# The second attention by pairs of heads, features on partitions, and a row norm that is applied to the output product

## The reference

```python
proj = einsum('bsd,de->bse', x, w_in)
q, k, v, z_att, z_ssm, xbc, dt_raw = split(proj)          # 16 heads of 64
# three dilated windows (1, 4, 16) of causal attention with a bias by distance, merged by their lse
y_att = wts[0] * o1 + wts[1] * o2 + wts[2] * o3
y_att = rms_norm_2(y_att * silu(z_att), att_norm_g)       # over the 1024 features of a token
y_ssm = rms_norm_2(y * silu(z_ssm), ssm_norm_g)           # the state part, in the same way
mix = concatenate([y_att, y_ssm], axis=-1)                # 2048 features
out = einsum('bse,ed->bsd', mix, w_out)
x = layer_norm(alpha * x + out, ln_g, ln_b)
```

## Time and profile before

| | us |
|---|---|
| median of 3 runs (lowest, highest) | 2261.53 (2259.41, 2262.16) |
| the profiled execution, its own time | 2260.03 |
| its span, first to last instruction | 2258.2 |
| TensorE busy | 2044.2 (91%) |
| VectorE, ScalarE, GpSimd busy | 1319.2, 765.9, 613.6 |
| second attention, first scores to the last product | 1464 to 2038 |
| norm and turns behind it | 2038 to 2065 |
| output product | 2065 to 2230 |
| rest of layer norm, last store | 2230 to 2258 |

### The profile page before, as it was taken

One profiled execution on the slowest core, in us unless ns is written; L12 is line 12 of the kernel. 1 busy time (PEld: TensorE's weight loads), 2 busy tenths in 40 slices (PEclk: granted clock), 3 DMA queues, 4 the chain that ended last, 5 costly groups with the idle time before them and its releaser, 6 DMA issues.

```text
span 2258.2 us, 30694 instructions
## 1 busy us (share of the span) xinstructions
PE 2044.2 (91%) x12412; PEld 1246.1 (55%) x12412; DVE 1319.2 (58%) x2349; ACT 765.9 (34%) x1446; POOL 613.6 (27%) x623
## 2 busy tenths in 40 slices
PE   2999889988999988696998999899999999998994
PEld 2433345444444555244444665566776677677884
DVE  6328999999973464315455888455455545564005
ACT  3313434443216664113212443333333333333003
POOL 0031425541842023755322225012201220120110
PEclk8999989998999999897999999999999999999997
DMA  7110111221311212214111002001100110012101
GB/s 317 38 47 24 43 38 61 71 70 61 150 38 61 89 38 94 112 38 166 40 38 38 1 1 75 24 16 38 38 35 4 38 38 18 21 38 94 47 30 75
DMA packets 18542, 129.95 MB, mean 58 GB/s; under 512 B 1760, under 2 KB 1760, under 8 KB 13024
## 3 DMA queue, kind: packets, MB, share of 16 engines
q1 hardware_dynamic: 12864, 99.67, 11.8%
q0 software_dynamic: 5536, 28.31, 3.2%
HBM read 109.10 MB, written 18.87 MB: 57 GB/s over the span
## 4 chain that ended last, share of the span: by engine, by line
PE 74%; DVE 14%; ACT 3%; POOL 3%; DMA 2%; issue 2%; SPq 0%; DVEq 0%; POOLq 0%; ACTq 0%
PE ps L768 45%; PE ps L765 7%; PE ps L803 5%; PE ps L828 3%; DVE arena L1436 3%; PE ps L817 3%; PE ps L866 2%; POOL arena L487 1%; PE ps L1039 1%; PE ps L1059 1%; PE ps L927 1%; PE ps L853 1%; POOL arena L617 1%; DMA W<-in_mods 1%; PE ps L974 1%
## 5 line engine op out<-in xcount | busy, mean ns | idle before, releaser
L768 PE MATMUL ps<-hT,W 128*128 128x512 bf16 x2688 | 629.6, 390 | 24.6 <-DVE arena L1454 11.2
L768 PEld LDWEIGHTS ps<-hT,W 128*128 128x128 bf16 x2688 | 257.5, 97 | 371.4 <-issue 17.6
L496 POOL TENSOR_TENSOR W<-W 128x512 bf16<-128x512 f32 x224 | 247.8, 1144 | 421.1 <-DMA W<-in_loads 420.7
L768 PE MATMUL ps<-W,arena 128*128 128x256 bf16 (+1 forms) x1920 | 264.1, 298 | 21.8 <-DVE arena L1824 19.8
L768 PE MATMUL ps<-W,hT 128*128 128x256 bf16 (+2 forms) x2112 | 278.1, 286 | 5.1 <-issue 3.3
L1468 DVE COPY arena<-ps 128x512 f32<-128x512 f32 (+1 forms) x192 | 105.5, 557 | 252.1 <-PE ps L803 246.4
L768 PEld LDWEIGHTS ps<-W,arena 128*128 128x128 bf16 x1920 | 186.7, 97 | 98.6 <-DVE arena L1824 20.3
L768 PEld LDWEIGHTS ps<-W,hT 128*128 128x128 bf16 x2112 | 189.9, 97 | 81.3 <-issue 3.9
L1225 ACT ACTIVATE arena<-arena,small 128x128 f32<-128x128 f32 (+7 forms) x128 | 99.3, 776 | 331.7 <-DVE small L1477 331.6
L487 POOL TENSOR_TENSOR arena<-arena 128x512 f32<-128x512 f32 (+1 forms) x80 | 131.0, 1637 | 223.1 <-ACT arena L1387 127.1
L803 PE MATMUL ps<-arena 128*128 128x64 f32 x1152 | 149.3, 267 | 0.0
(11 more groups left out here) (293 smaller groups left out, 2791.5 us busy)
## 6 DMA issues: line engine op xcount, KB each, us to landing
W<-in_loads SPq DMA_DIRECT2D x35, 2048.0 KB, 7.9
gates_scratch<-arena SPq DMA_DIRECT2D x32, 256.0 KB, 2.0
arena<-gates_scratch POOLq DMA_DIRECT2D x2, 4096.0 KB, 13.6
arena<-in_x SPq DMA_DIRECT2D x2, 2048.0 KB, 13.6
W<-in_mods SPq DMA_DIRECT2D x2, 2048.0 KB, 18.3
hT<-in_mods SPq DMA_DIRECT2D x2, 2048.0 KB, 28.9
arena<-in_x POOLq DMA_DIRECT2D x1, 4096.0 KB, 13.5
x_scratch<-arena POOLq DMA_DIRECT2D x8, 512.0 KB, 6.8
```

Of the source, the lines that this page charges most:

```text
L496: last = nc.gpsimd.tensor_tensor(low(v), v, high(v), ALU.subtract)
L768: last = mm(o, left[:, :, a], right[:, :, b], start=(k == first_k and (a, b) == PRODUCTS[0]), stop=(k == last_k and (a, b) == PRODUCTS[-1]))
```

## The change

The second attention goes over to `pair_attention`, the first layer's form, with 64 items of two heads (`items2`). `attention`, `low_parts`, `norm_rows` and POOL's gate go away. q, k and v of a pair come out whole by ACT, features on the partitions; v is turned by PE in two further units ("turned v", 4 transposes each) and comes out once more. z comes out as tanh by ACT and is multiplied by DVE (`pair_gate_made`). The pair's result stays with features on partitions (`pair_y`), so that its turns are gone: `pair_close` on ACT multiplies it with the gains into `mixA` and squares it; POOL sums the squares over the pairs (`y2_sum`) and makes the low part. The root of the mean square is a factor of a token: both norms are now applied to the output product, by rows. `turn_tiles` for `Z` so waits for the gated chunks alone, and pair 0's units lie between its turns. The output product is in two parts of 16 units with 512 columns and one row tile each: the state part (`woS0`, `woS1`) behind pair 0, ahead of the attention, taken out by ACT with the factor into `res`; the attention part (`woA0`, `woA1`) behind the attention, added by DVE with its factor. The residual x is loaded into `hT` and added to `res` by POOL. All is divided by `ALPHA`, which the layer norm does not see but for its epsilon.

In the attention a pair's 8 items now carry all 10 units of the next pair: `filler` is called at two places of each item, and the pair's units all use bank 0 (banks 2 to 5 hold scores, 6 and 7 transposes, 1 the output).

```diff
-    loads += [f"pair{j}" for j in range(8)] + [f"wo{j}" for j in range(4)]
+    loads += ["pair0", "woS0", "woS1"] + [f"pair{j}" for j in range(1, 8)] + ["woA0", "woA1"]
+PAIR_UNITS = (("q", 0), ("q", 1), ("k", 0), ("k", 1), ("v", 0), ("v", 1), ("turned v", 0), ("z", 0), ("turned v", 1), ("z", 1))
+BETWEEN_TURNS = tuple((i, share) for i in range(len(PAIR_UNITS))
+                      for share in ((BOTH,) if PAIR_UNITS[i][0] == "turned v" else (FIRST_HALF, SECOND_HALF)))
...
+    if UNITS[u][0][:4] == "pair":
+        return UNITS[u][1] % 2 if UNITS[u][0] == "pair0" else 0
...
-        items2 = [(h, i, i, h) for h in range(HEADS2) for i in range(NT)]
+        items2 = [(j, i, i, j) for j in range(HEADS2 // 2) for i in range(NT)]
...
+            def pair_done(j):
+
+                if j:
+                    pool.wait_ge(s_ysq, j + 1)
+                    nc.gpsimd.tensor_tensor(y2_sum, y2_sum, pair_y, ALU.add).then_inc(s_yacc, 1)
...
+                for half in range(2):
+                    pool.wait_ge(s_yg, 2 * j + half + 1)
+                    v = mixA[:, j, half * 512:half * 512 + 512]
+                    nc.gpsimd.tensor_tensor(low(v), v, high(v), ALU.subtract).then_inc(s_alow, 1)
...
+            for t in range(NT):
+                nc.gpsimd.tensor_tensor(res[:, t, :], res[:, t, :], hT[:, t, :], ALU.add).then_inc(s_xadd, 1)
+                pool.wait_ge(s_xadd, t + 1)
...
-            for u in range(FIRST["pair0"], FIRST["pair0"] + 2):
-                unit(u)
             pe.wait_ge(s_yo, 16)
-            turn_tiles(Z, s_nrm["ssm"][3], s_nrm["ssm"][4], s_nrm["ssm"][5])
...
+            between_turns(0)
+            between_turns(1)
+            turn_tiles(Z, s_gated, 8, s_nrm["ssm"][4], s_nrm["ssm"][5], lambda n: between_turns(n + 2))
             pe.wait_ge(s_nrm["ssm"][5], 16)
...
+            units("woS0")
+            units("woS1")
+
+            def next_pair(n, place):
+
+                j, i = n // 8 + 1, n % 8
+                if j < 8 and n < 64:
+                    u = FIRST[f"pair{j}"]
+                    if i < 6:
+                        unit(u + i, place)
+                    else:
+                        unit(u + 2 * i - 6 + place)
...
+            pe.wait_ge(s_free, unit_end("woS1"))
...
+            pe.wait_ge(s_att[1]["read"], 64)
+            wo = FIRST["woA0"]
+            pe.wait_ge(s_alow, 14)
+            for u in range(wo, wo + 4):
+                unit(u, 0)
+            pe.wait_ge(s_yacc, 7)
+            for t in range(NT):
+                last = mm(ps[:, 4, t:t + 1], y2_sum[:, t * P:(t + 1) * P], ones[:, 0:1], start=True, stop=True)
+            last.then_inc(s_nrm["att"][0], 1)
+            pe.wait_ge(s_alow, 16)
             for u in range(wo, wo + 4):
                 unit(u, 1)
...
+            def pair_close(j):
+
+                act.wait_ge(s_att[1]["read"], 8 * j + 8)
+                for half in range(2):
+                    span = slice(half * 512, half * 512 + 512)
+                    A(mixA[:, j, span], pair_y[:, span], ACT.Copy, scale=par("attg")[:, j:j + 1]).then_inc(s_yg, 1)
+                act.wait_ge(s_yg, 2 * j + 2)
+                A(pair_y if j else y2_sum, pair_y, ACT.Square).then_inc(s_ysq, 1)
...
-                    extra(n)
+                    extra(n, 0)
                     act.wait_ge(sems["inverse"], n + 1)
                     act.wait_ge(sems["exp"], 2 * n + 2)
                     for x in range(2):
                         t = tiles["rows"][n % 2][x][:, 0:keys]
                         A(t, t, ACT.Copy, scale=rden[:, (n % 2) * 2 + x:(n % 2) * 2 + x + 1]).then_inc(sems["scaled"], 1)
+                    extra(n, 1)
...
+            def next_pair(n, place):
+
+                j, i = n // 8 + 1, n % 8
+                if j < 8:
+                    u = FIRST[f"pair{j}"]
+                    if i >= 6:
+                        evac(u + 2 * i - 6 + place)
+                    elif place == 1:
+                        evac(u + i)
+                if place == 1 and i == 1 and j >= 2:
+                    pair_close(j - 2)
...
+            def close2(m, o):
+                j, i = m // 8, m % 8
+                if i == 0:
+                    dve.wait_ge(s_free, FIRST[f"pair{j}"] + len(PAIR_UNITS))
+                    if j:
+                        dve.wait_ge(s_ysq, j)
+                        dve.wait_ge(s_yacc, j - 1)
+                span = slice(i * P, (i + 1) * P)
+                return mult(pair_y[:, span], o, pair_gate(j)[:, span])
...
+                V.scalar_tensor_tensor(v, ps[:, unit_bank(u), :], inv[:, t:t + 1], v, ALU.mult, ALU.add).then_inc(s_free, 1)
...
+                if name == "woA1" and t >= 1:
+                    row_norm(t - 1)
             row_norm(7)
```

More of the change, by code:

```diff
@@ L751, in unit @@
                 spans = [(piece, some) for piece in pieces]
-                if name[:2] == "wo" and share is not None:
-                    both = operands(name, i)[1]
-                    spans = [(both[0], range(8, 16))] if share == 0 else [(both[0], range(8)), (both[1], range(16))]
                 for (cols, lhs, rhs), span in spans:
-                    first_k, last_k = 0, steps - 1
-                    if name[:2] == "wo" and share is not None and cols.start == 0:
-                        first_k, last_k = 8, 7
                     for k in span:
@@ L1169, in evac @@
                     j = int(name[4])
-                    if i == 0 and j >= 2:
-                        act.wait_ge(s_att[1]["read"], 2 * (j - 1))
-                    if i == 4 and j >= 1:
-                        act.wait_ge(s_zs, j)
-                    if i < 4:
-                        for h in range(2):
-                            own, other = slice(64 * h, 64 * h + 64), slice(64 - 64 * h, 128 - 64 * h)
-                            if i < 2:
-                                last = A(pq[j % 2][own, h, half], bank[own], ACT.Copy, scale=-ATTN_SCALE)
-                            else:
-                                A(pk_high[j % 2][own, h, half], bank[own], ACT.Copy)
-                                last = A(pk_high[j % 2][other, h, half], bank[own], ACT.Copy)
-                        last.then_inc(s_high, 1)
+                    what, h = PAIR_UNITS[i]
@@ L1410, in _, with between_turns @@
-            attention(s_att[1], items2, groups2, at2, next_pair)
-            pair_squares(7)
+            A(rss, rss, ACT.Sqrt).then_inc(s_nrm["ssm"][2], 1)
+            def between_turns(e):
+                i, share = BETWEEN_TURNS[e]
+                if share != FIRST_HALF:
+                    evac(FIRST["pair0"] + i)
+            between_turns(0)
+            between_turns(1)
+            for n in range(16):
+                act.wait_ge(s_nrm["ssm"][4], n + 1)
+                k, half = turned(n)
+                A(high(mixS[:, k, half * 512:half * 512 + 512]), ps[:, 4 + n % 4, :], ACT.Copy,
+                  scale=par("ssmg")[:, k:k + 1]).then_inc(s_mixh, 1)
+                between_turns(n + 2)
@@ new lines, in _ @@
+            inverse_roots(rss, s_nrm["ssm"][3], (s_nrm["ssm"][2], 1))
+            for n in range(16):
+                dve.wait_ge(s_mixh, n + 1)
+                k, half = turned(n)
+                v = mixS[:, k, half * 512:half * 512 + 512]
+                V.scalar_tensor_tensor(low(v), ps[:, 4 + n % 4, :], par("ssmg")[:, k:k + 1], high(v),
+                                       ALU.mult, ALU.subtract).then_inc(s_nrm["ssm"][5], 1)
+                i, share = BETWEEN_TURNS[n + 2]
+                if PAIR_UNITS[i][0] == "z" and share == SECOND_HALF:
+                    pair_gate_made(0, PAIR_UNITS[i][1])
```

432 lines of the change are left out of this document (163 added, 269 removed).

## The result

The changed kernel takes 2246.08 us (median of 7 runs, 2240.73 to 2251.45), the one before 2259.41 in the runs beside it (2255.63 to 2262.16). The ratio is 0.994, 95% interval 0.9923 to 0.9956: faster by 0.6%, 13.3 us. The profiled execution (its time 2240.73, span 2239.0) is the shortest of the seven, so its stages add up to more than the medians do.

What follows compares the result with a forecast made beforehand. PE was taken to bound the second attention, with DVE's layer norm rows behind it. Pair 0 -6.8, attention +14.9, tail -16.5 and layer norm -8.3 sum to -16.7 us: 2245 us from a median of 2261.5, range 2222 to 2267.

Steps and rivals of the forecast that it cites:

- Pair 0: Before the second attention: units and turns without the norm's wait, -6.8 us once the moved 86.7 us are set aside.
- the second z's wait: In pair 0, the second z waits for the first (table load, tanh, product): 1.5 us.
- Attention, prices: Second attention: block prices taken from the first attention give 72.4 us of PE work a period, against 75.98 before.
- rival B: Second attention: a second full-width filler piece costs tile-shape changes again, 0.36 to 0.46 us an item, +20 to +26; chance 0.12.
- Attention, waits: Second attention: PE waits for ACT's copy, 2.4 us at item 6, 2.6 at item 7; 5.7 us of waits a period.
- rival A: Second attention: all 14 new waits sink the clock at 1.7 us each, +24, giving 2269 us; chance 0.12.
- granted clock 1.00 in the periods: Sign for the second attention: no low clock within its periods; a clock under 0.97 would count as wrong.
- Rival C: Second attention: the two waits don't show as ACT copies earlier; period 72.5, -39, giving 2206 us; chance 0.07.
- The last pair: End of the second attention: no filler, so it goes by its own chain, 48.9 us (bounds 43 to 55).
- Tail, -16.5: From the attention's end to PE's end: norm, sixteen turns and their waits are gone, 175.2 us with the moved 86.7.
- end, -8.3: From PE's end to the span's end: layer norm rows start earlier, one tile per unit, 20.3 us instead of 28.6.
- Rival D: Tail: DVE finds the first row late by two units (reciprocal chain or POOL's adds), +10, giving 2255 us; chance 0.12.

Runs made afterwards that it cites:

- the nine kernels: The changed kernel and edits of it, with the same code up to the state part's last product, which ends between 1393.7 and 1399.8 us.
- Experiment 5: Changed kernel with all 16 turns of the state rows together behind pair 0's first unit, not between the halves of the units: 2252.1 us.
- Experiment 1: Changed kernel with ACT's copy of the turned v ahead of both exps in items 6 and 7: 2207.52 us (median of 4).
- experiment 2: Changed kernel with ACT's copy of the turned v between the two exps of items 6 and 7: 2223.26 us.
- experiment 3: Changed kernel with two added ACT copies of 512 keys between the exps and the copy of the turned v, items 6 and 7: 2294.14 us.
- experiment 6: Changed kernel with layer norm rows done by two again, as in the kernel before: 2253.66 us.
- experiment 4: Changed kernel with ACT scaling the rows of the second attention twice, first by 1.0: 2253.59 us.
- experiment 7: Changed kernel without the second head's products with v in the second attention for all key blocks but the first: 2250.89 us.

## Why the prediction was right

The median lies 1 us from the forecast and well inside the range, and most steps held by themselves. That it is as near as 1 us is in part luck: the runs of the kernel before that stand beside it have a median 2.1 us lower than the one known then, and the saving is 13.3 us where 16.5 were forecast. The steps are taken in its order.

**The unchanged part.** Predicted 0, measured -4.6 in one execution; by the spread of that product's end over the nine kernels this is chance. It is also why the predicted sum (-16.7) lies between that of the stages with it (-19.1) and without it (-14.5).

**Pair 0, -6.8, measured -8.5.** The start came 3.35 us behind the last product, as said (3.4), and the cold start cost 1.3 (6.70 us from the first of 24 matmuls to the next group against 5.42; predicted 1.8). The mis-sized term is the second z's wait: 1.5 in the sum, 0.26 measured, since with the turned v between the two, tanh and product are mostly done. Experiment 5 shows the interleaving to be worth 4.75.

**Attention, prices.** The sum of work was 72.4 us a period. Experiment 1, without the waits, gives 72.97, so the prices by block taken from the first attention were right to 1%. What is missing is mostly the second full-width filler piece of an item: between the products and the next scores it takes 2.82 us (from 1554.56 on, first period of the changed kernel), where the first, between scores and transposes, takes 2.71 (from 1558.45 on), 0.1 us an item. That is what is left of rival B, whose price was 0.36 to 0.46. In the prediction I cited the Trainium skill, TensorEngine Tiling (Array Packing), section Key Properties, with its rule that a change of tiling mode drains TensorE. The trace agrees so far as this border costs 0.1 us; whether a drain is what costs it, no run shows. One bound in the prediction is added up wrongly: ACT's second pass was put at "at most 8 x 2.2 = 16 us" a period, which is 17.6; by the lengths of the single scalings it is 11.5, and nothing in the sum hung on it.

**Attention, waits.** 2.4 and 2.6 us were predicted, 2.05 and 2.19 measured, at the place named and on the releaser named. Experiments 1 to 3 show that they cost their length, one for one, and are set by the copy's place in ACT's queue: at item 6 they are 0 ahead of the exps, 1.03 between them, 2.05 behind them, 3.52 with two more copies ahead of it. The 0.5 us for the second z and the 0.2 for the third unit are not there. Periods of undisturbed clock are 77.4 us (77.8 predicted): work 0.6 more, waits 1.0 less.

**Attention, the clock.** The forecast had none of rival A, and its sign "granted clock 1.00 in the periods" did not come in the four periods with a long unit (0.98). Four of the 14 units fell to a low clock, 1.5 us each, 6 us. This is the whole of what the attention took beyond the prediction (+18.3 against +14.9) and more, since the fast periods were 0.4 below theirs. Rival A's mechanism is real, and its price of 1.7 was near; only its count (14) was wrong. The unchanged attention had four such units in the trace of experiment 6 and six in that of experiment 5. At 1.5 us each, their number would make a part of the 11 us between the shortest and the longest run of the changed kernel; only one of the seven was looked at in that way.

**Rival C.** Its condition was that the copy comes earlier, its price a period of 72.5 and a kernel of 2206. The kernel as changed doesn't do it; experiment 1 does, and gives 72.97 and 2207.5.

**The last pair.** 48.9 predicted, 48.8 from its second step to the output product. ACT is on its chain (experiment 4). The nearness is luck in part: the prediction put nothing there for the clock, and with the low clock that experiments 1, 3 and 5 had, the same pair takes 2.1 to 2.4 us more.

**Tail, -16.5, measured -16.3, and end, -8.3, measured -8.0.** Both steps came as worked out: the product runs 88.8 us without a stop, rows are 5.98 us apart, the last store 5.8 behind the last row. Experiment 6 gives the end back (+9.4). Rival D did not happen: POOL's eight adds took 19.6 us from 2137.84 on and stayed ahead.

So the saving is made up as the prediction said: 33 us gained before and behind the attention (31.6 predicted), 18 given back inside it (14.9). That the giving back was needless, experiment 1 shows: with the copy moved by one place the attention is 16 us shorter than before the change, not 18 longer.

## What to carry to other kernels

When several producers are made to share one buffer, walk its release through the queue of the engine that empties it: what counts is not how long the copy takes (0.57 us here) but what stands ahead of it (two exps, 2.1 us), and an idle moment of that engine ahead of them may hold it for nothing. Count a wait on the bounding engine at its length plus a chance of a low clock behind it. Work added to an engine under cover should be priced apart for the stretch where the cover ends: here the last pair.

## What the runs showed of the hardware

**In the periods, a longer wait was followed by a low clock more often.** Behind 14 waits of 1.03 to 1.06 us no unit of 24 matmuls was long; behind 14 of 2.05 and 2.19 us, four (four as well in the traces of experiments 4 and 6, six in those of 5 and 7, so 24 of 70); behind 14 of 3.5 to 3.7, all. A drop cost 1.5 to 1.6 us where the unit began before or as the clock fell, and 2.5 where the clock had fallen ahead of it; I had put one price on all.

**Two heads beside each other in the array are one head's time.** This is for products of 64 outputs by 128 queries, the two heads in two halves of the array. Leaving out 448 of the second head's records changed the attention by 0.5 us, and four blocks took 1.09 us with 10 or 16 records.
